# The h projections of a hybrid encoder layer as Strassen pairs, with raw gates and queries kept in DRAM

## The chip, the cores and the metric

The kernel runs on one core of a Trainium2 chip. The metric is the device time of one execution in microseconds. All arithmetic that decides the result is float32: every large matrix product is made of three float32r matmuls (high part times high part, high times low, low times high), so each operand is first split into a high part (a copy to float32r) and a low part (the original minus the high part).

## The reference, cut to what matters

One layer, sequence 1024, width 1024:

```python
h = rms_norm(x, g_pre)
proj = h @ w_in          # 7424 columns = 58 tiles of 128
(a_b, a_c, a_x, a_z, b_q, b_k, b_v, b_z, m_q, m_z, gate_logits) = split(proj)
ya = short_gated_conv(a_b, a_c, a_x, w_conv) * silu(a_z);          ua = ya @ w_up_a
yb = window_attention_with_sink(rope(q), rope(k), v) * silu(b_z);  ub = yb @ w_up_b
ym = memory_cross_attention(m_q, mk, mv) * silu(m_z);              um = ym @ w_up_m
merged = g0 * ua + g1 * ub + g2 * um       # g = sigmoid(gate_logits), 3 x 1024 channels
out = x + rms_norm(merged @ w_out, g_post)
```

Every product must keep float32 quality. The 58 tiles of `h @ w_in` are three quarters of the large matmuls; three up projections (24 tiles with half the depth) and the output projection (8 blocks) are most of the rest.

## The kernel before, in words

Everything is written out by hand: each engine has one in-order program, and semaphores tie them together. There is no planner and no due time; the place of an instruction in its engine's program is its priority.

Channels lie on partitions, positions along the free axis. `h_hi` and `h_lo` hold the normalized input for all of the kernel's first 920 us. A tile of 128 output channels is computed by `product` (L360 to L383): for both halves of the sequence and each of the eight chunks of the depth it issues three matmuls (L377, L378, L379), 48 in all, into `pm[:, p]`, one of two PSUM tiles. The weights of a tile arrive in `raw[:, p]` (512 KB), ScalarE makes the high part (`split_next`, L635 to L638) and GpSimd the low part (`low_part`, L336 to L341, the subtraction is L340), both a whole tile ahead of TensorE.

The stages come in this order: transposition of the normalized x under the first tile (`turn_x`, L398); K, V and four Q tiles, with rotation on VectorE (L944 to L947); 16 conv tiles (`conv_tiles`, `conv_z`, VectorE lines L961 to L978); eight rounds of `merge_a`, each a gate tile and an up tile with two groups of window attention among the matmuls (scores L458 and L459, `softmax_head` L1011, `softmax_tail` L1024 to L1027, transposition of the probabilities L466, `take_probs` L746 and L1034, values L480); z and memory queries; keys and values of the memory (L541, L555); eight rounds of `merge_b` with the cross-attention; the z and gate tiles of the third branch; and eight output blocks (`out_block`, L617 to L619). A gate tile is used at once: its sigmoid is taken from PSUM, and VectorE multiplies it with the up tile that follows. Queries, keys and values stay in SBUF. What VectorE and ScalarE take from PSUM they take a tile at a time (128 x 1024).

SyncE issues nearly all DMAs in order: weights, x, the swapped rows of one attention block at a time (`move_qk`), and the output. VectorE's program in `merge_a` and ScalarE's program in `merge_a` are one fixed sequence per round.

## Time and profile before

| | us |
|---|---|
| time, median of 3 runs (1020.91 to 1022.86) | 1021.28 |
| the profiled execution, its own time | 1020.34 |
| its span | 1018.3 |

| engine | busy, us | share of the span |
|---|---|---|
| TensorE matmul (PE) | 990.7 | 97% |
| weight load (PEld) | 824.7 | 81% |
| VectorE (DVE) | 474.3 | 47% |
| ScalarE (ACT) | 347.5 | 34% |
| GpSimd (POOL) | 167.6 | 16% |

The span is the time from the first to the last instruction of the profiled execution; the time of the execution is 2.0 us longer. Matmuls are pipelined, so the busy time of one overlaps the next: the distance between the starts of two of them, not the duration, is what one costs. An engine's busy time includes time in which an instruction has started and is held up.

### The profile page before, as it was taken

The numbers are of one execution on the slowest core, as the hardware profiler recorded it, in microseconds if no ns is written. First come the engines' busy times: TensorE is split into PE (matmuls) and PEld (weight loads), VectorE is DVE, ScalarE is ACT, GpSimd is POOL, SyncE is SP. The second block draws the span as 40 slices with busy tenths as digits, with TensorE's granted clock in tenths as the row PEclk, the third lists the DMA queues.
The fourth block names the chain that finished last, engine by engine and source line by source line (L and its number), as shares of the span: only waits on it lengthen the run. The fifth ranks groups of instructions, "written<-read, shape, count | busy, mean of one in ns | idle before, by whom it ended". The sixth has DMA issues, their size and how long they took to land.

```text
span 1018.3 us, 12976 instructions
## 1 busy us (share of the span) xinstructions
PE 990.7 (97%) x4672; PEld 824.7 (81%) x4672; DVE 474.3 (47%) x896; ACT 347.5 (34%) x567; POOL 167.6 (16%) x85
## 2 busy tenths in 40 slices
PE   4999999999999999999999999999999999999997
PEld 3788888888878888888888888888888888887885
DVE  5524322245477777774555544334435312127343
ACT  6321131211365555553320344434422211115121
POOL 1112122121111111111220011121122112210000
PEclk9999999999999999999999999999999999999999
DMA  6322111112111111111121410011111111160322
GB/s 224 107 51 53 62 41 62 41 41 70 32 50 50 50 49 49 49 39 62 41 84 62 135 62 31 31 51 38 44 42 45 49 31 62 31 257 0 124 82 83
DMA packets 21339, 65.41 MB, mean 64 GB/s; under 512 B 3232, under 2 KB 4384, under 8 KB 21056
## 3 DMA queue, kind: packets, MB, share of 16 engines
q1 hardware_dynamic: 20992, 64.39, 19.0%
q10 hardware_dynamic: 320, 0.66, 0.4%
q8 instruction: 18, 0.29, 0.1%
q14 instruction: 9, 0.07, 0.0%
HBM read 56.51 MB, written 4.19 MB: 60 GB/s over the span
## 4 chain that ended last, share of the span: by engine, by line
PE 84%; DVE 7%; ACT 4%; issue 3%; DMA 1%; DVEq 0%; SPq 0%; ACTq 0%
PE pm L377 22%; PE pm L379 22%; PE pm L378 22%; PE pm L617 3%; PE pm L619 3%; PE pm L618 3%; ACT area_a L738 2%; PE sa L466 2%; PE pv L589 1%; PE pm L541 1%; PE sa L573 1%; PE pv L480 1%; DVE area_a L1027 1%; DVE units_r L1034 1%; PE sa L458 1%
## 5 line engine op out<-in xcount | busy, mean ns | idle before, releaser
L377 PE MATMUL pm<-h_hi,units_r 128*128 128x512 f32 x928 | 364.0, 392 | 3.0 <-DVE h_lo L935 2.8
L379 PE MATMUL pm<-h_hi,units_r 128*128 128x512 f32 x928 | 361.7, 390 | 0.0
L378 PE MATMUL pm<-h_lo,units_r 128*128 128x512 f32 x928 | 361.7, 390 | 0.0
L340 POOL TENSOR_TENSOR units_r<-units,units_r 128x1024 fp32r<-128x1024 f32 x80 | 166.4, 2080 | 731.9 <-ACT units_r L638 731.9
L377 PEld LDWEIGHTS pm<-h_hi,units_r 128*128 128x128 f32 x928 | 174.5, 188 | 39.3 <-DVE h_lo L935 3.4
L379 PEld LDWEIGHTS pm<-h_hi,units_r 128*128 128x128 f32 x928 | 174.5, 188 | 36.5
L378 PEld LDWEIGHTS pm<-h_lo,units_r 128*128 128x128 f32 x928 | 174.6, 188 | 35.2
L638 ACT ACTIVATE units_r<-units 128x1024 fp32r<-128x1024 f32 x90 | 91.7, 1019 | 198.1 <-PE pm L379 172.2
L1179 DVE TENSOR_TENSOR area_a<-area_a,pm 128x1024 f32<-128x1024 f32 x15 | 18.3, 1221 | 139.5 <-PE pm L379 139.5
L377 PE MATMUL pm<-y_hi,units_r 128*128 128x512 f32 x192 | 76.9, 401 | 0.0
L379 PE MATMUL pm<-y_hi,units_r 128*128 128x512 f32 x192 | 75.0, 390 | 0.0
L378 PE MATMUL pm<-y_lo,units_r 128*128 128x512 f32 x192 | 74.8, 390 | 0.0
L617 PE MATMUL pm<-h_hi,units_r 128*128 128x512 f32 x128 | 50.0, 391 | 0.3 <-DVE h_lo L1226 0.2
L618 PE MATMUL pm<-h_hi,units_r 128*128 128x512 f32 x128 | 49.9, 389 | 0.0
L619 PE MATMUL pm<-h_lo,units_r 128*128 128x512 f32 x128 | 49.8, 389 | 0.0
L379 PEld LDWEIGHTS pm<-y_hi,units_r 128*128 128x128 f32 x192 | 36.0, 188 | 7.7
L1034 DVE TENSOR_TENSOR units_r<-sa,area_a_r 128x512 fp32r<-128x512 f32 x48 | 30.2, 684 | 24.9 <-ACT area_a_r L746 24.9
L378 PEld LDWEIGHTS pm<-y_lo,units_r 128*128 128x128 f32 x192 | 36.1, 188 | 6.7
L377 PEld LDWEIGHTS pm<-y_hi,units_r 128*128 128x128 f32 x192 | 36.1, 188 | 6.7
L746 ACT ACTIVATE area_a_r<-sa 128x512 fp32r<-128x512 f32 x48 | 25.2, 599 | 41.1 <-PE sa L466 41.1
L738 ACT ACTIVATE area_a<-area_a,st 128x384 f32<-128x384 f32 x64 | 38.4, 602 | 0.0
L837 ACT ACTIVATE area_a<-pm 128x1024 f32<-128x1024 f32 x8 | 8.2, 1027 | 74.5 <-PE pm L379 74.5
(154 smaller groups left out, 1037.9 us busy)
## 6 DMA issues: line engine op xcount, KB each, us to landing
units<-in_w SPq DMA_DIRECT2D x58, 512.0 KB, 3.3
units<-in_wup SPq DMA_DIRECT2D x24, 256.0 KB, 2.6
area_m<-in_x SPq DMA_DIRECT2D x8, 512.0 KB, 7.0
units<-in_wmem SPq DMA_DIRECT2D x8, 512.0 KB, 3.2
area_a<-in_wout SPq DMA_DIRECT2D x2, 2048.0 KB, 10.5
units<-in_x SPq DMA_DIRECT2D x8, 512.0 KB, 3.9
out<-area_a SPq DMA_DIRECT2D x7, 512.0 KB, 2.9
area_a_r<-area_m SPq DMA_DIRECT2D x16, 128.0 KB, 2.3
```

What stands on the lines that cost most here:

```text
L340: nc.gpsimd.tensor_tensor(w_lo[:, p, 0:width], raw[:, p, 0:width], w_hi[:, p, 0:width].bitcast(F32), ALU.subtract).then_inc(lo_made, 1)
L377: pe.matmul(pm[:, p, cols], hi, src_hi[:, k, cols], start=(k == 0), stop=False)
L378: pe.matmul(pm[:, p, cols], hi, src_lo[:, k, cols], start=False, stop=False)
L379: mm = pe.matmul(pm[:, p, cols], lo, src_hi[:, k, cols], start=False, stop=(k == chunks - 1))
L466: mm = pe.transpose(sa[:, bank, h * P:(h + 1) * P], probs[:, h, j * P:(j + 1) * P], ident[:, :])
L617: pe.matmul(dst, hi, wo_hi[:, n * HALF:(n + 1) * HALF], start=(k == 0), stop=False)
L618: pe.matmul(dst, lo, wo_hi[:, n * HALF:(n + 1) * HALF], start=False, stop=False)
L619: mm = pe.matmul(dst, hi, wo_lo[:, n * HALF:(n + 1) * HALF], start=False, stop=(k == KC - 1))
L638: nc.scalar.activation(w_hi[:, p, 0:width], raw[:, p, 0:width], ACT.Copy).then_inc(hi_made, 1)
L738: ins = nc.scalar.activation(probs[:, h, :], probs[:, h, :], ACT.Exp, bias=st[:, 3, h:h + 1], accum_out=st[:, 5, h:h + 1])
L746: nc.scalar.activation(probsT_hi[:, j, :], sa[:, bank, :], ACT.Copy).then_inc(pt_hi_made, 1)
L1034: nc.vector.tensor_tensor(probsT_lo[:, j, :], sa[:, bank, :], probsT_hi[:, j, :].bitcast(F32), ALU.subtract).then_inc(pt_lo_made, 1)
```

## The change

The projections of h are computed in pairs of tiles. A pair is a product of a 2x2 block matrix of weights (two tiles, each cut at half the depth: A11, A12 for the first, A21, A22 for the second) with a 2x2 block matrix of h (depth cut in two, sequence cut in two). Strassen's scheme in Winograd's form needs seven block products in place of eight. Each block product is 4 chunks times 3 matmuls of 128x512, so 12 matmuls. The 58 tiles make 29 pairs.

- h is kept as seven blocks `hc`, four of them sums (T1 to T4), each with high and low part; they are made once, after x is transposed. VectorE makes the sums, ScalarE the high parts, GpSimd and VectorE the low parts.
- Per pair, GpSimd makes four sums of weight blocks (S1, S3 in the place of A21, S2, S4), 128x512 each, and seven low parts; ScalarE seven high parts. The ring holds four operands, so operand n+4 may be made once product n is done.
- Seven PSUM results per pair, each a bank (128x512), are combined into four output blocks: ScalarE copies the first (`take_a`), VectorE adds the others with seven instructions that read PSUM.
- The order of work is new: K, Q and V pairs; z, gate and memory-query pairs for all branches, with the 16 groups of window attention one per pair in pairs 4 to 19; 16 memory steps; then the eight conv pairs, with the eight rounds of cross-attention one per pair; then all 24 up projections; then the output blocks, as before.
- Raw gates, raw z tiles and raw memory queries (pairs 3 to 20) are stored in DRAM and read back; rotated q and k, and the outputs of both attentions, too. SyncE issues all of it in order.

The products of a pair run in the order P1, P2, P6, P7, P4, P5, P3. TensorE puts the values of attention group gr - 1 (and of cross round i - 1) ahead of P2, the scores ahead of P6, and the transposition of the probabilities ahead of P3. ScalarE makes the high part of operand n + 4 after product n, and then runs `exps` after P6 and `take_probs` after P5. VectorE's program for one pair is, in order:

- after P1: `rotate` (pairs 2 and 3), `take_output(gr - 1)`, `conv_b`, `stage_mq(i)`;
- after P2: `take_c11`, `softmax_head(gr)` or `take_cross`, `cross_max(i)`;
- after P6: `add_p6`, then `rope_low`, `conv_y`, or in pair 20 `scale_mem`;
- after P7: `add_p7`, then `rotate`, `softmax_tail(gr)` or `cross_norm(i)`;
- after P4: `take_c21`, in pair 20 `split_mem`; after P5: `take_c22` and one more addition, `take_probs(gr)`; after P3: `take_c12`, then `conv_taps` in every second conv pair.

```diff
+HC = KC // 2
+H_OF = {"P1": B11, "P2": B21, "P3": B22, "P4": T4, "P5": T1, "P6": T2, "P7": T3}
+W_OF = {"P1": A11, "P2": A12, "P3": S4, "P4": A22, "P5": S1, "P6": S2, "P7": A21}
+def slot_order():
+    order = [(0, "P1"), (0, "P2"), (1, "P1"), (1, "P2")]
+    order += [(p, name) for p in range(2) for name in ("P6", "P7", "P4", "P5", "P3")]
+    for p in range(2, PAIRS):
+        if p == P_CONV:
+            order += [("m", i) for i in range(M_STEPS)]
+        order += [(p, name) for name in ("P1", "P2", "P6", "P7", "P4", "P5", "P3")]
...
@@ block.gpsimd
+            for n in range(8, NS):
+                p, name = ORDER[n]
+                low_part(n)
+                if name == "P3" and p < P_LAST:
+                    sums_first(p + 1)
+                elif name == "P1":
+                    sum_s2(p)
+                elif name == "P2":
+                    sum_s4(p)
...
@@ block.tensor
+            def product(n, moving_hi, moving_lo, bank, ready=None):
+                pe.wait_ge(hi_made, n + 1)
+                pe.wait_ge(lo_made, n + 1)
+                for k in range(HC):
+                    pe.matmul(bank, hi, moving_hi(k), start=(k == 0), stop=False)
+                    pe.matmul(bank, hi, moving_lo(k), start=False, stop=False)
+                    mm = pe.matmul(bank, lo, moving_hi(k), start=False, stop=(k == HC - 1))
...
@@ block.scalar
+            def high_part(n):
+                wait_operand(act, n)
+                at_least(act, slot_done, n - RING + 1)
+                nc.scalar.activation(ring[:, n % RING, 0, :], operand(n), ACT.Copy).then_inc(hi_made, 1)
...
@@ block.vector
+            def take_c21(p):
+                wait_slot(dve, p, "P4")
+                dve.wait_ge(c_made, p + 1)
+                nc.vector.tensor_tensor(raw_block(p, 1, 0), bank_of(p, "P4"), snaps[:, 2, :], ALU.add).then_inc(c21, 1)
...
@@ block.sync
+            for g in range(UPS):
+                if g >= 2:
+                    load_gate(g)
+                if g + 4 < UPS:
+                    sp.wait_ge(lo_made, NS + g + 1)
+                    sp.dma_start(spots[:, g % 4, :], wup[g + 4]).then_inc(spot_landed[g % 4], 16)
+                if g < 2:
+                    load_y(g + 2)
```

## Rows read from the trace of the kernel before

**Rows 1.** The page: span, busy time, and the chain by engine.

```profile
span 1018.3 us, 12976 instructions
PE 990.7 (97%) x4672; PEld 824.7 (81%) x4672; DVE 474.3 (47%) x896; ACT 347.5 (34%) x567; POOL 167.6 (16%) x85
...
PE 84%; DVE 7%; ACT 4%; issue 3%; DMA 1%; DVEq 0%; SPq 0%; ACTq 0%
```

**Rows 2.** Windows: stretch, its length, PE busy (count), clock, DMA share, GB/s.

```profile
26.50:72.10 45.60, 45.58 (x221) 1.00 0.26 80
...
480.00:560.00 80.00, 80.00 (x363) 1.00 0.20 66
640.00:700.00 60.00, 60.00 (x316) 1.00 0.12 39
```

**Rows 3.** Timeline of PE, 472 to 480 us: start, duration, line.

```profile
472.43 0.40 PE L377 MATMUL pm<-h_hi,units_r 128*128 128x512 f32 x1
...
479.92 0.39 PE L377 MATMUL pm<-h_hi,units_r 128*128 128x512 f32 x1
```

**Rows 4.** Windows of one attention round, all engines: PE PEld DVE ACT POOL.

```profile
304.00:329.51 25.51, 25.27 (x127) 20.94 (x126) 19.54 (x63) 14.70 (x31) 3.68 (x2) 1.00 0.19 50
```

**Rows 5.** Chain in order of time, near 60 us: start, length, what.

```profile
60.36 0.87 PE sa L431 x8
```

**Rows 6.** Groups by form: busy us, mean ns | idle before, releaser.

```profile
L340 POOL TENSOR_TENSOR units_r<-units,units_r 128x512 fp32r<-128x512 f32 x23 | 29.7, 1289 | 75.1 <-ACT units_r L638 75.1
...
L638 ACT ACTIVATE units_r<-units 128x512 fp32r<-128x512 f32 x8 | 5.0, 631 | 4.7 <-PE pm L379 4.7
...
L1034 DVE TENSOR_TENSOR units_r<-sa,area_a_r 128x512 fp32r<-128x512 f32 x48 | 30.2, 684 | 24.9 <-ACT area_a_r L746 24.9
L1027 DVE TENSOR_SCALAR area_a<-area_a,st 128x384 f32<-128x384 f32 x64 | 22.5, 416 | 0.6
```

**Rows 7.** Timeline of POOL and DVE near 204 us.

```profile
203.86 2.40 POOL L340 TENSOR_TENSOR units_r<-units,units_r 128x1024 fp32r<-128x1024 f32 x1 [6.22 <-ACT units_r L638]
...
202.83 1.23 DVE L961 TENSOR_TENSOR area_m<-pm,area_m 128x1024 f32<-128x1024 f32 x1 [13.77 <-PE pm L379]
204.18 2.63 DVE L963 TENSOR_SCALAR area_m<-area_m,wconv 128x1024 f32<-128x1024 f32 x1
```

**Rows 8.** Timeline of POOL and DVE near 795 us.

```profile
795.12 1.28 POOL L340 TENSOR_TENSOR units_r<-units,units_r 128x512 fp32r<-128x512 f32 x1 [8.41 <-ACT units_r L638]
...
784.69 3.10 DVE L1106 TENSOR_TENSOR area_a<-area_a 128x1024 f32<-128x1024 f32 x1
795.51 1.97 DVE L1106 TENSOR_TENSOR area_a<-area_a 128x1024 f32<-128x1024 f32 x1 [0.16 <-DVE area_a L1103]
```

**Rows 9.** Timeline, 8 to 12 us: two DVE instructions and one of POOL.

```profile
8.27 1.42 DVE L921 TENSOR_SCALAR area_m<-area_m,st 128x1024 f32<-128x1024 f32 x2
...
11.31 3.50 DVE L921 TENSOR_SCALAR area_m<-area_m,st 128x1024 f32<-128x1024 f32 x2
11.45 2.80 POOL L340 TENSOR_TENSOR units_r<-units,units_r 128x1024 fp32r<-128x1024 f32 x1 [11.00 <-ACT units_r L638]
```

**Rows 10.** Timeline of POOL and DVE near 317 us; ACT and DVE of one softmax.

```profile
316.05 2.39 POOL L340 TENSOR_TENSOR units_r<-units,units_r 128x1024 fp32r<-128x1024 f32 x1 [20.64 <-ACT units_r L638]
317.33 1.89 DVE L1034 TENSOR_TENSOR units_r<-sa,area_a_r 128x512 fp32r<-128x512 f32 x3 [1.63 <-ACT area_a_r L746]
...
322.09 0.60 ACT L738 ACTIVATE area_a<-area_a,st 128x384 f32<-128x384 f32 x1
324.61 0.58 ACT L752 COPY area_a<-pv 64x512 f32<-64x512 f32 x1
...
327.54 1.41 DVE L1027 TENSOR_SCALAR area_a<-area_a,st 128x384 f32<-128x384 f32 x4
```

**Rows 11.** DMA issues: size and median time from issue to landing.

```profile
units<-in_w SPq DMA_DIRECT2D x58, 512.0 KB, 3.3
units<-in_wup SPq DMA_DIRECT2D x24, 256.0 KB, 2.6
```

More of the change, by code:

```diff
@@ L18 @@
-from contextlib import ExitStack, contextmanager
+from contextlib import ExitStack
 import numpy as np
@@ L86, in link @@
     def link(self, ins):
[L88 removed]
+        self.count += 1
         ins.then_inc(self.sem, 1)
[L90 to L103 removed]
+        self.eng.wait_ge(self.sem, self.count)
@@ L436, in conv_tile, with turn_v @@
-            def conv_tile(j, q, first=0, last=None):
-                product(2 * j + (T_CONV + q) // 2, q % 2, KC, h_hi, h_lo, 4 * j + (T_CONV + q + 1), first, last)
-            with pe.Fori(0, AC - 1) as j:
-                for q in range(4):
-                    conv_tile(j, q)
-            def scores(i, g):
+            def turn_v(half):
+                pe.wait_ge((c11, c12)[half], 3)
+                if half == 0:
+                    pe.wait_ge(h_copied, 2 * KC)
+                for b in range(4):
+                    mm = pe.transpose(sa[:, half, b * P:(b + 1) * P], raw_block(2, 0, half)[:, b * P:(b + 1) * P],
+                                      ident[:, :])
+                mm.then_inc(v_turned, 1)
@@ L625, in _ @@
-            out_block(0, 1)
-            with pe.Fori(1, NB // 2 - 1) as i:
-                for p in range(2):
-                    out_block(i, p)
-            out_block(NB // 2 - 1, 0)
-            out_block(NB // 2 - 1, 1, last=True)
+                        hi, lo = mb[:, p, 0, k, :], mb[:, p, 1, k, :]
+                        wo = wo_of[half]
+                        pe.matmul(dst, hi, wo[:, k, 0, :], start=(k == 0), stop=False)
+                        pe.matmul(dst, lo, wo[:, k, 0, :], start=False, stop=False)
@@ L633, in _ @@
+                        mm = pe.matmul(dst, hi, wo[:, k, 1, :], start=False, stop=(k == KC - 1))
+                    if half == 0 and b == NB - 1:
+                        mm.then_inc(out_half_done, 1)
+                mm.then_inc(out_done, 1)
+            for b in range(NB):
+                out_block(b)
         @block.scalar
         def _(act):
-            def split_next(p, t_half, width=D):
-                act.wait_ge(raw_landed[p], 16 * t_half + 16)
-                nc.scalar.activation(w_hi[:, p, 0:width], raw[:, p, 0:width], ACT.Copy).then_inc(hi_made, 1)
@@ L888, in _ @@
-            with act.Fori(1, NB // 2 - 1) as i:
-                for p in range(2):
-                    out_block(i, p, True)
-            out_block(NB // 2 - 1, 0, False)
-            out_block(NB // 2 - 1, 1, False, last=True)
         @block.vector
@@ L1190, in merge_b, with cross_norm @@
                                         ALU.mult).then_inc(mnm_ready, 1)
-                if after is not None:
-                    stage_mq(after)
+            def cross_norm(i):
                 dve.wait_ge(mexped, i + 1)
```

2010 lines of the change are left out of this document (1192 added, 818 removed).

## The prediction

> **What bounds the kernel now.** I read the page first, then windows, then TensorE's own timeline, then what GpSimd and VectorE do to one another. The page gives TensorE 97% busy and 84% of the chain [rows 1]. Busy is no proof, since matmuls overlap, so the windows come next: whole stretches have PE busy for every microsecond of their length at the full clock [rows 2]. The timeline gives the price: from 472.43 to 479.92 there are 33 steps from start to start, 7.49 / 33 = 0.227 us for a 128x512 matmul, and no step longer than that [rows 3]. A tile of 48 costs 10.88. The kernel is TensorE's issue rate almost everywhere; the other engines have 50% and more to spare [rows 1]. A change that removes matmuls gains exactly what it removes, if all that now has to be ready for each product is ready.
>
> **What is removed.** 58 tiles x 48 = 2784 matmuls become 29 x 7 x 12 = 2436. 348 x 0.227 = **-79 us**. Up projections, output blocks, memory products, scores, transpositions and values keep their numbers. This is the full prize, 7.7%.
>
> **What is added, per pair.** TensorE: 84 x 0.227 = 19.0. GpSimd: seven low parts and four sums of 128x512, 11 x 1.29 [rows 6] = 14.1; in an old round of 25.5 us it had 3.7 [rows 4]. VectorE: seven additions from PSUM at 0.68 (row of L1034) [rows 6] = 4.8. ScalarE: seven copies at 0.63 [rows 6] and one from PSUM, 5.0. Sums of busy time all fit below 19. In an attention pair the group adds to TensorE what it did before: an old round is 72 h and up matmuls, 16.3 us, of 25.51 [rows 4], so 4.6 for a group with its waits, and the pair is 23.6. Throughput alone hides everything. What decides is latency in VectorE's fixed order, and there the trace has something that the old kernel could ignore.
>
> **The lock.** At 204.18 a 128x1024 tensor_scalar of VectorE on SBUF data takes 2.63 us; the GpSimd subtraction that started at 203.86 ends at 206.26, and only 0.55 is left after it [rows 7]. At 795.51 an SBUF-only tensor_tensor takes 1.97, where GpSimd's 128x512 instruction of 1.28 started just ahead of it; at 784.69, in the same step of a tile with a 128x1024 low part, it takes 3.10 [rows 8]. Operations that read PSUM go through untouched: L1034 at 317.33 needs 1.89 for three inside a GpSimd instruction [rows 10]. So a VectorE instruction that reads only SBUF waits for the whole GpSimd instruction. And it goes in turns: with nothing in the way two tensor_scalars take 1.42; at 11.31 two take 3.50, while GpSimd's 11.45 start takes 2.80 in place of 2.39, that is 0.41 to wait for the first of them, and then the second waits for all of GpSimd's [rows 9]. If GpSimd has a queue of work, each SBUF-only VectorE instruction costs its own time plus up to 1.29.
>
> The Trainium skill says the same (SBUF — State Buffer, "Who interferes with whom"): a VectorE instruction with two SBUF inputs, or in a two-port mode, and a GpSimd instruction that reads SBUF exclude each other for their full length. By that page the tiny 128x4 tensor_tensor at the head of `softmax_tail` is held too; the trace of before has none of them beside a GpSimd instruction. By the rule the stall below is 3.4 a pair, without it 1.9.
>
> **Attention pairs (16).** Time 0 is the end of P2. TensorE: scores to 1.4, with a wait for the first mask (VectorE has `take_c11`, 0.7, ahead of it) to 1.8; P6 to 4.5, P7 to 7.2, P4 to 10.0, P5 to 12.7, and then the transposition of the probabilities wants `p_ready`. ScalarE: after P6 a high part to 5.2, then the exponentials, 322.09 to about 324.6 in the old trace, 2.5 [rows 10], so exped at 7.8. VectorE: `add_p7` to 8.05, then `softmax_tail`. GpSimd in that stretch: low part of P3 5.3 to 6.6, S1 to 7.9, S3 to 9.25, and behind it without a gap the low part of P1, S2, the low part of P2, S4, the low part of P6: eight instructions in a row. The tail's four tensor_scalars, 1.41 together when free [rows 10], 0.35 each, now alternate with them: if the 128x4 operation is free, 9.25 + 4 x 0.35 + 3 x 1.29 = 14.5; if it is held too, one more turn, 16.1. TensorE stands from 12.7 to there: 1.9 or 3.4. Lower bound 0 (VectorE keeps the lock for all four), upper 4.8 (the reciprocal also takes a turn). I take 2.6, the middle of the two cases that the rows allow: 16 x 2.6 = **+42** (0 to 77). The mask wait is about the old round's bubbles and is not counted again. Behind the stalled transposition only P3 waits on TensorE; on VectorE `take_c21` and `take_c22` come late, but their banks are wanted three products on.
>
> **The opening, pairs 0 to 3.** Before, four tiles were done at 72.1: tile 2 ends at 60.36, then 0.87 and one tile [rows 5]. After, seven blocks of h must be made. GpSimd has ten low parts of them, nine operands and the sums of two pairs, in one order: P2 of pair 0 can start only after 4 block lows and 5.5 us of such work; P6 of pair 0 needs all of h, then VectorE's twelve SBUF additions of 0.7, then their high and low parts; from there each product needs two block lows and one low part of GpSimd, 3.9 us against 2.7. I get P6 of pair 0 at 49, P3 of pair 0 at 68, pair 1 at 85. That is 13 behind the old kernel where 5 ahead would be the full gain: 18. Pairs 1 to 3 then carry five rotations of three 1.2 us SBUF operations and one low part each, all under the lock, and each waits for four row DMAs that SyncE starts only when the tile is complete (an old load of 256 KB takes 2.6 [rows 11]): VectorE gets behind by a product or two and TensorE waits for banks, 5 to 8 more. From the bound where only the GpSimd rate counts to one where every rotation is a full turn late: 10 to 30; I take **+22**.
>
> **The memory steps.** `scale_mem` in pair 20 is five tiny operations and two tensor_scalars beside the same GpSimd queue, wanted 2.7 after P6: 7 late at worst. The 16 steps need a copy, a low part and a load each of about 1.4 in turn with TensorE. +6 (0 to 12).
>
> **The conv pairs (8).** `cross_norm` is four tensor_scalars in the same place: 1.7 late. In every second pair `conv_y` (two SBUF operations) is ahead of it: 4. `conv_taps` (four SBUF operations, 4.4 free, two or three turns held) stands ahead of `stage_mq`, and the next scores wait for that behind P2, 7.2 after P3: 2 late, three times. Together up to 27; if turns are lost only half the time, 13. **+20** (4 to 35).
>
> **The end.** Loads of z and attention output for the third y tile wait for `y_lo_made`, and the gate load stands behind them in SyncE's order. ScalarE takes that gate's sigmoid before the y tile's: up projection 4 starts about 5 late. One or two more after the last up. **+7** (2 to 14). The stores to DRAM lie beside other work: a pair moves 1 MB of weights and 1 MB of raw blocks in 19 us, about 110 GB/s; 80 GB/s took a share of 0.26 of the DMA engines [rows 2], so this would be some 0.36.
>
> **Sum.** 1018.3 - 79 + 42 + 22 + 6 + 20 + 7 = 1036.3 of span. The profiled execution's own time is 2.0 above its span and the median 0.9 above that: **1039**.
>
> **The rivals.** (a) The lock is taken once and kept: VectorE's queued instructions follow one another, so a tail waits once and ends at 10.7, before TensorE wants it. Then attention costs 0, conv 7, the opening 18, the memory steps 4 and the end 5: 1021 - 79 + 34 = 976. If a tail still loses one turn of 1.29 in half of the 27 places where one can, and attention's first mask 0.45 in 16, it is 976 + 17 + 7 = 1000. Between them, nearer the second, **993**. For it: the alternation rests on one place [rows 9]. Against it: there GpSimd plainly got in between. This one is faster; it decides at about 1.3 us of stall per attention pair, where the sum meets 1021. (b) Everything is hidden as the busy sums suggest and only the opening costs its lower bound: 1021 - 79 + 10 = **952**. For it: busy sums below 19 per pair. Against: the order. (c) More turns are lost than I count (reciprocal held, `take_c12` late, TensorE's clock falling in gaps: matmuls now never leave 1.00 in the windows [rows 2]): attention +77 and opening +30 in the sum above: 1039 + 35 + 8 = **1082**.
>
> **Chances.** Forecast 0.54 (1018 to 1076), (a) 0.28, (b) 0.05, (c) 0.13. Range: from 982 to 1080. The forecast's own range is 1018 to 1076. A measurement here can tell 0.2% from no change: 1019.2 to 1023.3 is same, 0.04, mostly from the bottom of the forecast. Faster 0.32, slower 0.64.
>
> **What would show it.** In the trace after: the transposition of the probabilities idle for 2 to 3 us each of 16 times, released by `softmax_tail`'s tensor_scalar; that instruction's mean well above 0.42, with GpSimd instructions between its four; pair 1 complete near 85 us, pair 4 near 135; gaps ahead of cross scores in every second conv pair; a gap of some 5 us at the fifth up. Wrong would be: tensor_scalars of the tail at 0.35 with GpSimd at work (then the lock is no matter), PE without gaps from 100 to 800 us, or gaps released by GpSimd itself, whose 14.1 a pair would then be longer than I read it.

## The result and the profile after

| | before | after |
|---|---|---|
| median of four runs, us | 1021.25 (1020.91 to 1022.86) | 1063.94 (1063.22 to 1065.82) |
| span of the profiled execution, us | 1018.3 | 1064.0 |
| ratio | | 1.0418, 95% interval 1.0400 to 1.0436 |

The kernel got 4.2% slower, by 42.7 us. The forecast was 1039 us, 1.7% slower, by 18: the direction and the range held, the size did not. Of the executions of all kernels in this document one, of the first run of section 7, was slow (1201 us at a granted clock of 0.745); it is in that run's median, and the ratios leave it out.

The page after, in the lines that answer to [rows 1], with the row of TensorE's granted clock in 40 slices of the span:

```profile
span 1064.0 us, 12467 instructions
...
PE 942.7 (89%) x4324; PEld 774.2 (73%) x4324; DVE 648.7 (61%) x1012; ACT 385.7 (36%) x736; POOL 542.0 (51%) x386
...
PEclk9778898999999999999999999999999798999999
...
PE 27%; DVE 10%; issue 4%; DMA 2%; ACT 2%; POOL 1%; SPq 0%; DVEq 0%; ACTq 0%
```

348 matmuls are gone, and TensorE is no longer busy all the time. The chain says less than it seems to: the profile follows it back only to 569 us, and its shares add up to 46% of the span, so TensorE's 27% is some 59% of what was followed, where before it had 84 of 99. No other engine is busy for more than 61%. So the question is who makes TensorE wait. The table of TensorE's waits from 28 us on (who waits, for whom: us in total, times, longest) answers it:

```profile
PE pm L675 <- POOL ring L589: 31.0, 8, 10.6
PE sa L740 <- DVE area L1369: 15.2, 16, 1.5
PE pm L907 <- DVE area L1591: 14.8, 2, 8.2
PE sa L818 <- DVE area L1421: 8.1, 8, 1.7
PE pm L675 <- DVE area L1240: 8.0, 2, 7.7
PE pm L907 <- POOL ring L589: 4.0, 3, 3.1
PE sa L810 <- DVE area_r L1407: 3.7, 3, 1.2
PE sa L732 <- DMA area_r<-kl_d: 3.7, 1, 3.7
PE pm L937 <- DVE hc L1580: 3.5, 1, 3.5
PE sa L784 <- DVE area_r L1398: 3.3, 1, 3.3
PE sa L732 <- DVE st L1354: 3.1, 15, 0.2
...
```

L675 is the first matmul of an h product, L907 of an up projection, L937 of an output block; L740 and L818 are the transpositions of the probabilities (attention, cross-attention), L732 and L810 the scores, L784 a memory step. Before, the same view from 28 us on has 4.8 us in all. Read by stage, TensorE waited 39 us and more for the h products of the opening, 18 in attention and 22 at the end.

The turns of the two engines are there as the forecast read them from [rows 7 to 9]. Timeline of VectorE and GpSimd at the tail of one softmax:

```profile
248.46 0.15 DVE L1366 TENSOR_TENSOR st<-st 128x4 f32<-128x4 f32 x1
248.65 0.18 DVE L1367 RECIPROCAL st<-st 128x4 f32<-128x4 f32 x1
248.86 5.25 DVE L1369 TENSOR_SCALAR area<-area,st 128x384 f32<-128x384 f32 x4
...
247.15 1.30 POOL L602 TENSOR_TENSOR spots<-spots 128x512 f32<-128x512 f32 x1
248.53 1.29 POOL L604 TENSOR_TENSOR spots<-spots 128x512 f32<-128x512 f32 x1
249.78 1.41 POOL L589 TENSOR_TENSOR ring<-spots,ring 128x512 fp32r<-128x512 f32 x1
251.15 1.40 POOL L610 TENSOR_TENSOR spots<-spots 128x512 f32<-128x512 f32 x1
252.51 1.39 POOL L589 TENSOR_TENSOR ring<-spots,ring 128x512 fp32r<-128x512 f32 x1
253.86 1.39 POOL L618 TENSOR_TENSOR spots<-spots 128x512 f32<-128x512 f32 x1
```

Four tensor_scalars that took 1.41 us [rows 10] take 5.25, one for each boundary between two of GpSimd's instructions. The groups by line (busy, mean ns); the first had a mean of 416 in [rows 6]:

```profile
L1369 DVE TENSOR_SCALAR area<-area,st 128x384 f32<-128x384 f32 x64 | 83.3, 1360 | 0.6
...
L1421 DVE TENSOR_SCALAR area<-area,st 128x256 f32<-128x256 f32 x32 | 36.9, 1213 | 0.3
```

In the opening and at the end the timeline (PE, then DVE, then POOL) shows longer gaps, and matmuls 0.43 us apart behind them instead of 0.23:

```profile
53.89 0.77 PE L675 MATMUL pm<-hc,ring 128*128 128x512 f32 x1 [10.62 <-POOL ring L589]
54.45 0.63 PE L676 MATMUL pm<-hc,ring 128*128 128x512 f32 x1
54.88 0.63 PE L677 MATMUL pm<-hc,ring 128*128 128x512 f32 x1
...
59.19 13.58 DVE L1302 TENSOR_TENSOR hc<-area,hc 128x512 fp32r<-128x512 f32 x8
115.31 1.23 DVE L1322 TENSOR_TENSOR area<-area 128x1024 f32<-128x1024 f32 x1 [8.05 <-DMA area<-area]
824.04 1.23 DVE L1567 TENSOR_TENSOR area<-area 128x1024 f32<-128x1024 f32 x1 [9.57 <-DMA area<-ob_d]
844.83 1.37 DVE L1569 TENSOR_TENSOR area<-area,snaps 128x1024 f32<-128x1024 f32 x1 [8.02 <-ACT snaps L1145]
...
97.27 1.26 POOL L602 TENSOR_TENSOR spots<-spots 128x512 f32<-128x512 f32 x1 [8.09 <-DMA spots<-in_w]
```

L1302 is a low part of a block of h, L1322 a rotation that waits for its swapped rows, L1567 and L1569 a y tile at the end, L602 the first weight sum of a pair. The gap of 10.62 is the one ahead of P6 of pair 0.

### The profile page after: what moved, and what is told of

It reads as the page before. It is cut to its first block and busy times, and to the rows that moved or that the text cites. A ratio compares the mean times of both kernels' runs of the same rounds, so it can differ in the third digit from the quotient of the medians.

```text
span 1064.0 us, 12467 instructions
## 1 busy us (share of the span) xinstructions
PE 942.7 (89%) x4324; PEld 774.2 (73%) x4324; DVE 648.7 (61%) x1012; ACT 385.7 (36%) x736; POOL 542.0 (51%) x386
## 5 line engine op out<-in xcount | busy, mean ns | idle before, releaser
L589 POOL TENSOR_TENSOR ring<-spots,ring 128x512 fp32r<-128x512 f32 x227 | 323.8, 1429 | 319.9 <-ACT ring L952 319.7
L675 PE MATMUL pm<-hc,ring 128*128 128x512 f32 x812 | 326.9, 403 | 40.2 <-POOL ring L589 31.0
L676 PE MATMUL pm<-hc,ring 128*128 128x512 f32 x812 | 321.3, 396 | 0.0
L677 PE MATMUL pm<-hc,ring 128*128 128x512 f32 x812 | 320.9, 395 | 0.0
L952 ACT ACTIVATE ring<-spots 128x512 fp32r<-128x512 f32 x227 | 141.9, 629 | 331.4 <-PE pm L677 299.6
L675 PEld LDWEIGHTS pm<-hc,ring 128*128 128x128 f32 x812 | 156.0, 192 | 75.9 <-issue 34.5
L677 PEld LDWEIGHTS pm<-hc,ring 128*128 128x128 f32 x812 | 155.4, 191 | 33.8
L676 PEld LDWEIGHTS pm<-hc,ring 128*128 128x128 f32 x812 | 156.0, 192 | 30.3
L907 PE MATMUL pm<-hc,ring 128*128 128x512 f32 x192 | 78.4, 409 | 18.8 <-DVE area L1591 14.8
L1369 DVE TENSOR_SCALAR area<-area,st 128x384 f32<-128x384 f32 x64 | 83.3, 1360 | 0.6
L908 PE MATMUL pm<-hc,ring 128*128 128x512 f32 x192 | 77.6, 404 | 0.0
L909 PE MATMUL pm<-hc,ring 128*128 128x512 f32 x192 | 77.3, 402 | 0.0
L907 PEld LDWEIGHTS pm<-hc,ring 128*128 128x128 f32 x192 | 37.8, 197 | 28.6 <-issue 20.8
L937 PE MATMUL pm<-hc 128*128 128x512 f32 x128 | 49.9, 390 | 3.5 <-DVE hc L1580 3.5
L938 PE MATMUL pm<-hc 128*128 128x512 f32 x128 | 49.8, 389 | 0.0
L939 PE MATMUL pm<-hc 128*128 128x512 f32 x128 | 49.8, 389 | 0.0
L602 POOL TENSOR_TENSOR spots<-spots 128x512 f32<-128x512 f32 x29 | 41.7, 1439 | 13.2 <-DMA spots<-in_w 13.0
L1136 ACT ACTIVATE area<-area 128x1024 f32<-128x1024 f32 x24 | 25.4, 1057 | 62.8 <-DMA area<-raw_d 62.8
L1240 DVE TENSOR_TENSOR area<-pm,snaps 128x512 f32<-128x512 f32 x29 | 20.0, 690 | 42.4 <-PE pm L677 35.7
L1251 DVE TENSOR_TENSOR snaps<-pm,snaps 128x512 f32<-128x512 f32 x29 | 20.0, 689 | 40.8 <-PE pm L677 40.6
L1245 DVE TENSOR_TENSOR snaps<-pm,snaps 128x512 f32<-128x512 f32 x29 | 20.0, 691 | 39.6 <-PE pm L677 39.1
```

The lines of the kernel that those rows point to most:

```text
L589: nc.gpsimd.tensor_tensor(ring[:, n % RING, 1, :], operand(n), ring[:, n % RING, 0, :].bitcast(F32), ALU.subtract).then_inc(lo_made, 1)
L675: pe.matmul(bank, hi, moving_hi(k), start=(k == 0), stop=False)
L676: pe.matmul(bank, hi, moving_lo(k), start=False, stop=False)
L677: mm = pe.matmul(bank, lo, moving_hi(k), start=False, stop=(k == HC - 1))
L907: pe.matmul(dst, hi, y[:, at, 0, cols], start=(begin and c == chunks[0]), stop=False)
L908: pe.matmul(dst, hi, y[:, at, 1, cols], start=False, stop=False)
```

## The experiments

Every one starts from the changed kernel. A ratio is to the kernel before on the same chip, where the changed kernel stands at 1.0418; the times of single events are those of the profiled execution. TensorE's first scores start at 164.09 us in the changed kernel and its up projections, from the last values of the cross-attention (806.64) to the end of the last (966.55), take 159.9 us, where 24 x 24 matmuls at 0.227 are 130.8. Both vary where the edit doesn't touch them: in the eight profiled executions that have the changed kernel's opening as it is, the first scores start between 160.7 and 164.1, and in seven that have its end as it is, the up projections take 159.7 to 164.0. Differences inside of these spreads are read as none.

### 1. The divisions by the softmax sum on ScalarE

```diff
@@ softmax_tail, VectorE
-    for h in range(GROUP):
-        ins = nc.vector.tensor_scalar(probs[:, h, :], probs[:, h, :], st[:, 6, h:h + 1], None, ALU.mult)
@@ ScalarE, after P7
+    for h in range(GROUP):
+        ins = nc.scalar.activation(probs[:, h, :], probs[:, h, :], ACT.Identity, scale=st[:, 6, h:h + 1])
```

> The four tensor_scalars that divide the probabilities by their sums move from VectorE to ScalarE (activations with a scale), where nothing takes turns with GpSimd's weight sums. Theory (turns with the weight sums): in the changed kernel those four take 5.25 us from the first to the last where VectorE's own pace was 416 ns each, and TensorE stands 0.92 us at the transposition and 0.2 us at the scores in each of 16 attention pairs; with them gone the pairs lose that, so about -19 us, period 24.81 -> about 23.6 us, and GpSimd's low sums beside them fall from about 1.40 to 1.29 us. Rival (the stall is the order or the latency of the chain, not the turns): the activation takes its own time behind the exponentials and the high sums, so the stall stays or grows, 0 to +10 us.

Measured: 1048.49 us, ratio 1.0263 (1.0226 to 1.0300); span 1044.3, so 19.7 less. The transposition waits for nothing any more, while each operation takes 606 ns on ScalarE against 1360 in turns (groups by line):

```profile
L1045 ACT ACTIVATE area<-area,st 128x384 f32<-128x384 f32 x64 | 34.2, 606 | 0.3
L741 PE MATMUL sa<-ident,area 128*128 128x128 f32 x192 | 23.6, 272 | 0.0
```

The turns held TensorE in the attention pairs. They cost 15.2 us of waits, 15.5 in the median times and 19.7 in the spans of the two profiled executions, so 15 to 20 us. The 0.2 us at the scores (3.1 in all) stayed.

### 2. GpSimd's weight sums 4 columns wide

```diff
-    nc.gpsimd.tensor_tensor(spots[:, S1, :], spots[:, A21, :], spots[:, A22, :], ALU.add)
+    n = HALF if p == 0 else 4
+    nc.gpsimd.tensor_tensor(spots[:, S1, 0:n], spots[:, A21, 0:n], spots[:, A22, 0:n], ALU.add)
```

and the same for S3, S2 and S4.

> GpSimd's four weight sums of a pair cover 4 columns in place of 512 for pairs 1 to 28 (the products of those pairs are not the reference's; all else runs as before). Theory (what is slow in the changed kernel is VectorE taking turns with GpSimd, whose work the sums have grown from 2 to 3 operations of 1.3 us a product's worth): the 16 attention pairs lose their 0.92 and 0.2 us stalls (-18), the conv pairs part of 15.6 us (-8 to -12), the opening and the end little (0 to -6): -26 to -36 us. Rival (the turns are with the low parts of the weights, which stay, and the sums only stand beside them): 0 to -8 us, the 0.92 us stalls stay.

Measured: 1042.05 us, ratio 1.0197 (1.0163 to 1.0230); span 24.1 less, where 26 to 36 were expected. With seven low parts and no sums in a pair, the tail's mean fell to half and TensorE's wait for it from 15.2 to 0.5; the first scores start at 161.7, and the up projections did not get shorter:

```profile
L1369 DVE TENSOR_SCALAR area<-area,st 128x384 f32<-128x384 f32 x64 | 40.1, 687 | 0.6
```

So the sums make the attention stall, the low parts alone don't. Of the 24 us, 15 are that wait and 6 the same wait in the conv pairs (8.1 to 1.7); in the opening and at the end no cost of the sums shows.

### 3. The conv pairs

```diff
@@ cross_norm: as in experiment 1, on ScalarE
@@ VectorE, after P1
     if 1 <= i:
         stage_mq(i)
+    if 1 <= i < NB - 1 and i % 2 == 1:
+        conv_taps(p - 1)
@@ VectorE, after P3
-    if 0 <= i < NB - 2 and i % 2 == 0:
-        conv_taps(p)
```

> In the eight conv pairs the four tensor_scalars that divide the cross attention's probabilities (2.7 us for two in turns with GpSimd, 349 ns each before) move to ScalarE, and the raw query's staging goes ahead of the convolution's taps on VectorE. Theory (turns at the division, staging behind the taps): the 1.24 us gaps ahead of the scores and the 0.65 to 1.24 us gaps ahead of the transposition go, 15.6 us of loss falls to 3 to 6: -9 to -13 us. Rival (VectorE's sum of work in turns fills those pairs, so a gap moves to another wait): -3 to +3 us.

Measured: 1054.43 us, ratio 1.0326 (1.0309 to 1.0344), span 11.4 less; the time fell by 9.5, as the theory had it. Between 614 and 800 us TensorE waited 10.0 us in the changed kernel; here it is this (waits):

```profile
PE pv L831 <- issue: 0.8, 1, 0.8
PE sa L819 <- ACT area L1065: 0.3, 1, 0.3
```

### 4. TensorE's clock kept up

```diff
+BUSY_OPEN = {(0, "P2"): 28, (0, "P6"): 44, (0, "P5"): 30, (2, "P1"): 24, (3, "P1"): 20}
+BUSY_UP = {2: 34, 4: 26, 11: 0}
+    def keep_busy(count, bank, idx):
+        for _ in range(count):
+            pe.matmul(bank, hc[:, idx, 0, 0, 0:P], hc[:, idx, 0, 0, :], start=True, stop=True)
```

> TensorE is given matmuls without use (28, 44, 30, 24, 20 of them, 128x512) in five of the opening's gaps and two (34 and 26) in the up projections' gaps, before the matmul that waits; nothing else changes and their results are not read. Theory (part of the loss is TensorE at the lower of its clock levels after each gap: about 62 us of its work run at the lower level, 31 us of which would not be spent at the full one): the granted clock stays near 1 behind those gaps, matmuls 0.217 instead of 0.43 us apart, and the kernel gets up to 31 us shorter, half of that if VectorE or GpSimd end the next wait anyway: -10 to -31 us. Rival (VectorE and GpSimd bound those stretches, the slow matmuls were hidden behind them): the gaps grow by what the clock gives back, -3 to +3 us.

Measured: 1064.96 us, ratio 1.0414 (1.0393 to 1.0435): nothing. The clock did stay up in most of the gaps (page), and behind such a gap the matmuls are 0.23 apart (timeline); the first scores at 161.0 are within the spread:

```profile
PEclk9999998999999999999999999999999899998999
...
101.14 0.47 PE L677 MATMUL pm<-hc,ring 128*128 128x512 f32 x1 [0.79 <-POOL ring L591]
101.45 0.40 PE L678 MATMUL pm<-hc,ring 128*128 128x512 f32 x1
101.68 0.40 PE L679 MATMUL pm<-hc,ring 128*128 128x512 f32 x1
```

In the changed kernel TensorE is busy for some 47 us at the lower of its two levels (the expectation had 62), here for some 30, and the time did not follow. The waits come back at the next operand: P7 of pair 0 waits 2.23 us for GpSimd at 59.30, where it waited 0.58. The theory, 10 to 31 us, falls; a gain of a few us, hidden in the runs' spread, is not ruled out.

### 5. The opening: three orders and one size

Loads and rotations in another order:

```diff
@@ VectorE, pairs 2 and 3: rotate(j) of side 1 moves from P1 to P2, behind take_c11
@@ SyncE: load_spot(A22, 2) and load_spot(A22, 3) go ahead of swap_rows
```

> In the opening, VectorE rotates the second halves' queries after the results of the odd block product are taken instead of ahead of them (there it stood 8.05 and 7.99 us for the DMAs that swap the rows), and the loads of pair 2's and pair 3's last weight blocks are issued ahead of SyncE's row swaps (GpSimd waited 8.09 us for the first of them). Theory (a transfer issued late, behind a wait on its queue, makes half of the opening's gaps): the gaps of 6.04 and 5.04 us ahead of pairs 2 and 3 fall away, and with them the half-speed stretches behind them (about 3.4 us of work each), so -12 to -20 us. Rival (in the opening only the turns of VectorE and GpSimd count; both engines have more work than TensorE there): the gaps come back later, -3 to +3 us.

Measured: 1067.42 us, ratio 1.0445 (1.0417 to 1.0472). A gap of 6.10 us is back at 105.99, the others became 1.82 and 2.20. The first scores at 161.2 are within the spread, so nothing was won. The rival was right.

All low parts of the combinations on VectorE:

```diff
@@ GpSimd: low_of_combination(T2, T3, T4, T1, B22; j = 0, 2) removed
@@ VectorE
-    for j in (1, 3):
+    for j in range(HC):
         low_of_combination(nth + 1, idx, place, j)
```

> In the opening VectorE forms all low parts of the five combinations of h (20 in place of 10), GpSimd none. With the two engines taking turns a pair of such operations takes 1.71 us (1.29 of them GpSimd's), while VectorE alone starts one every 0.60 us. Theory (between 51 and 73 us the turns set the pace): VectorE's stretch of 21.7 us (14 operations, each with one of GpSimd's) becomes 24 x 0.60 plus turns with four low parts of weights, about 17 us, so the 7.73 us gap ahead of the second pair shrinks by 4 to 5 us; -4 us for the kernel, -8 with what follows at the higher clock level. Rival (the products of pair 0 wait for each combination's low part on one engine longer): 0 to +5 us.

Measured: 1067.34 us, ratio 1.0456 (1.0437 to 1.0474). The gap grew from 7.73 to 13.17; it stands ahead of P5 of pair 0, which waits for VectorE's addition of pair 1's first result (L1240). GpSimd, free of its low parts, went on to the next pair's sums (L602 to L618), and VectorE took turns with those: 1.21 us a piece in place of the 0.60 that I had reckoned with (timeline):

```profile
56.51 19.41 DVE L1302 TENSOR_TENSOR hc<-area,hc 128x512 fp32r<-128x512 f32 x16
...
64.72 1.70 POOL L602 TENSOR_TENSOR spots<-spots 128x512 f32<-128x512 f32 x1
66.51 1.59 POOL L604 TENSOR_TENSOR spots<-spots 128x512 f32<-128x512 f32 x1
```

ScalarE's rounding of the rotated tiles later, on top of the first of these orders:

```diff
@@ ScalarE: rope_high of side 1 from P2 to P6, of side 0 from P7 to P4; rope_high(0) from P6 to P7
@@ VectorE: rope_low and the second rotate, SyncE: store_rope, one or two products later too
```

> In the opening, on top of the rotations and loads in the other order (that run gained 2.9 us at the first scores), ScalarE rounds the rotated tiles one or two products later, VectorE and SyncE follow. There ScalarE stood 8.15, 6.35, 9.53 and 8.62 us at a rotated tile, with the rounding of the next weights queued behind it, and GpSimd 6.67, 6.64 and 2.77 us for those. Theory (the coupling of the queues): the gaps of 6.15, 1.83, 2.61 and 1.14 us ahead of pairs 2 to 4 shrink to 0 to 2 in all, the first scores start at 152 to 156 us in place of 164, -8 to -12 us for the kernel. Rival (VectorE and GpSimd in turns, or the landing of the swapped rows, bound it): the gaps come back at another product, the first scores start at 160 or later, -4 to 0 us.

Measured: 1067.35 us, ratio 1.0456 (1.0438 to 1.0475), first scores at 162.29. The gap of 6.1 fell to 4.06, and a new one of 3.02 came from VectorE. The rival again: the gaps came back elsewhere, though the kernel got 3 us slower where it had 0 to 4 less.

The rotations 4 columns wide:

```diff
-    link(nc.vector.tensor_tensor(raw, raw, cosb, ALU.mult))
+    link(nc.vector.tensor_tensor(raw[:, 0:4], raw[:, 0:4], cosb[:, 0:4], ALU.mult))
```

and so the two others and the four transfers of swapped rows.

> In the changed kernel the five rotations of the key's and queries' tiles, and the transfers that swap their rows, cover 4 columns in place of 1024 (keys and queries are not the reference's); all waits and their order stay, and so do the two roundings and the stores. Theory (VectorE's 15 operations of 1.2 to 2.3 us, of which each also holds GpSimd's for a turn, set the pace of pairs 1 to 3): the gaps of 6.04 and 5.05 us shrink below 2 in all and their half-speed stretches go, first scores at 148 to 154 us in place of 164, -10 to -16 us. Rival (the fixed latency of the transfers and the queues' order, which 4 columns do not change): first scores at 160 or later, 0 to -4 us.

Measured: 1053.62 us, ratio 1.0324 (1.0308 to 1.0339), first scores at 150.80. The gaps of 6.04 and 5.05 are now 1.25 and 2.11, and TensorE's waits for GpSimd up to the first scores are these, against 31.0:

```profile
PE pm L675 <- POOL ring L589: 23.3, 7, 10.6
```

So the size of the rotations, on VectorE in turns and in the transfers, is worth 10 to 13 us of the opening (10.3 in the median times, 13.3 at the first scores, 9.9 against the earliest of the untouched openings), and the two orders tried are worth nothing. Whether VectorE's operations or the transfers make it, the run doesn't tell. The gaps of 10.6 and 7.7 us at 54 and 75 us were taken away by no run (those with the busy TensorE only filled them, and the low parts on VectorE turned 10.6 and 7.7 into 9.3 and 13.2). They stand where the seven blocks of h are made, ahead of P6 and of P5 of pair 0; what would shorten them stays open.

### 6. The end

The product with the gate ahead of the y tiles:

```diff
@@ VectorE: gate_up(g) ahead of y_tile and wo_low; ScalarE: y_tile a step later
@@ SyncE: load_gate(2), load_gate(3) ahead of load_y(2), load_y(3)
```

> At the end VectorE forms the gate times up tiles ahead of the output's y tiles rather than behind them, ScalarE's part of y comes a step later, and the loads of the third and fourth raw gates are issued ahead of the loads of y. Theory (the gaps of 8.21, 6.57 and 3.14 us in the up projections and the 14.5 us between them and 130.6 + 1 us are order: gate_up stands behind a y tile that waits for its own transfers): gaps and the half-speed work behind them go, -12 to -25 us. Rival (the transfers of raw gates and weights are short of DMA time there, whatever the order): -3 to +3 us.

Measured: 1083.16 us, ratio 1.0605 (1.0579 to 1.0631), 19 worse, outside of both. The first gaps got shorter (2.15, 3.15), but there are now six waits in the first branch, 17.9 us in all in place of two of 14.8, and three in the second, 15.1 in all, with 8.08 and 6.73 at 911 and 925. I read it so, and no run shows it: each load of y waits in SyncE's queue for a place that is now free a step later, and the next raw gate's load stands behind it.

The y tiles spread over the steps, and loads issued as early as their places allow:

```diff
 def y_step(g):
-    if g < AC:
-        return g
-    return g - 5 if KC < g <= KC + AC else None
+    return {1: 0, 2: 1, 4: 2, 6: 3, 9: 4, 10: 5, 12: 6, 14: 7}.get(g)
@@ SyncE: load_gate(0), load_gate(1), load_y(0), load_y(1) ahead of store_cross(NB - 1)
```

> At the end SyncE issues the raw gates' and y tiles' loads before it waits for the last cross output (they stood behind a wait that ended at 814.5 us, while their places were free at 808.4), and the eight y tiles are formed at up steps 1, 2, 4, 6, 9, 10, 12, 14 in place of 0 to 3 and 9 to 12, so that the first product with a gate no longer stands behind a y tile. Theory (order and latency of the raw tiles' way back: 27.5 us are lost in the up projections): the 8.21 us gap falls to 0 to 2, the 6.57 us gap goes, the 3.1 us gaps of steps 10 and 11 shrink; -14 to -22 us. Rival (the sum of transfers from 815 to 870 us is what takes the time, DMA share 0.6 to 0.9): the gaps come later, 0 to -5 us.

Measured: 1062.52 us, ratio 1.0392 (1.0369 to 1.0416). The 8.21 us gap is 0.69, and 3.15, 4.77, 2.81 us come later: up projections still 158, and 1.4 us less for the kernel where the theory had 14 to 22. That looked like the transfers.

28 loads narrow, those of the raw gates and of the raw factors of y; only the gates' are shown:

```diff
-    sp.dma_start(gate[:, g % 2, :], raw_d[GATE[g // KC] + g % KC - T_GA])
+    w = 2 * HALF if g < 2 else 64
+    sp.dma_start(gate[:, g % 2, 0:w], raw_d[GATE[g // KC] + g % KC - T_GA][:, 0:w])
```

> At the end the raw gates from the third on and the raw factors of y from the third on come back 64 columns wide in place of 1024 (28 loads of 512 KB less; what the up projections are multiplied with is not the reference's). All waits and their order stay. Theory (the time of the transfers that the change adds: seven spread-out y tiles gained nothing, so it isn't the y tiles' place): the up projections take 135 to 142 us in place of 158, -14 to -22 us for the kernel. Rival (order: a raw gate's load is issued only when a y tile's low part is made, and small transfers don't change that; or VectorE's and GpSimd's own work in turns): -2 to -6 us.

Measured: 1062.52 us, ratio 1.0394 (1.0368 to 1.0421), up projections 156.5. The up projections are some 3 us below the spread where 135 to 142 were expected, so the size of these transfers is not what holds them; the attention outputs' loads kept their size. What is left is order, or the engines' work in turns. SyncE's own waits in the run with the spread tiles say where (waits from 804 to 910 us):

```profile
SPq L529 <- POOL hc L654: 43.2, 6, 12.1
SPq L516 <- DVE area L1588: 16.6, 5, 7.3
```

L529 is `load_y`, waiting for a place of y; L516, `load_gate`, comes behind it in the queue, and waits for VectorE itself too.

Loads of y a step later still (steps 1, 2, 5, 6, 9, 10, 13, 14, loads two steps after a tile; the cut is against the spread tiles above):

```diff
-    if g and y_step(g - 1) is not None and y_step(g - 1) + 2 < 2 * AC:
-        load_y(y_step(g - 1) + 2)
+    if g >= 2 and y_step(g - 2) is not None and y_step(g - 2) + 2 < 2 * AC:
+        load_y(y_step(g - 2) + 2)
```

> As the run with the y tiles spread over the up steps, and on SyncE a y tile's load is issued a step later still (steps 3, 4, 7, 8, 11, 12), so that the wait for a place of y no longer stands ahead of the next raw gate's load: there SyncE stood from 816.9 to 826.4 us with gate 3 behind it, which landed at 835 and let VectorE wait 7.6 us. Theory (head of line on SyncE): the gaps of 3.15, 4.77, 2.81 us and those of 3.4 and 1.8 us at steps 9 and 10 shrink to half, up projections 145 to 150 us in place of 158: -8 to -13 us against the changed kernel. Rival (two places for raw gates, whose load starts only when VectorE has taken the gate two steps before, are too few beside 4.4 us a transfer, whatever the queue's order): -2 to +2 us.

Measured: 1060.23 us, ratio 1.0376 (1.0350 to 1.0402), up projections 152.7: 7 us less where 8 to 13 were expected, and half of that reached the kernel's time.

The three queues untied:

```diff
@@ VectorE
     if y_step(g) is not None:
         y_tile(y_step(g))
-    if wo_step(g) is not None:
-        wo_low(wo_step(g))
     gate_up(g)
+    if wo_step(g) is not None:
+        wo_low(wo_step(g))
@@ ScalarE: y's sigmoid, then wo_high, then y's rounding (was: sigmoid, rounding, wo_high)
@@ SyncE: wup[4], wup[5] ahead of load_y(0); the first y tiles at steps 2 and 3
```

> At the end, on top of the y tiles spread over the up steps and their loads a step later: VectorE forms the gate times up before the output weights' low part, ScalarE rounds the output weights before y, the weights of up steps 4 and 5 are loaded ahead of the y tiles (ScalarE waited 8.33 us for them with a y tile's sigmoid queued behind), and no y tile stands ahead of step 2. Theory (three in-order queues wait for each other in each step: y's sigmoid, y, its rounding, the output weights' rounding and low part, then the product with the gate): the gaps of 2 to 4.2 us fall to 0 to 1.5, the up projections take 136 to 145 us in place of 158, so -13 to -20 us. Rival (transfers of a raw gate with two places only): 150 us or more, -3 to -8.

Measured: 1049.96 us, ratio 1.0274 (1.0242 to 1.0307), up projections 142.3. TensorE's waits from 806 us on fell from 23.1 to 10.1:

```profile
PE pm L933 <- DVE hc L1581: 3.5, 1, 3.5
PE pm L903 <- DVE area L1594: 2.4, 1, 2.4
PE pm L903 <- DVE area L1592: 2.3, 3, 1.7
PE pm L903 <- POOL hc L657: 1.1, 2, 0.7
```

Here the theory holds, and its number too. The run holds the moved loads of the one before; against that run, 1060.23, it gained 10.3. It changes four things at once, and which of them counts no run tells.

### 7. Together

Experiments 1 and 3, the first of the opening and the fourth of the end:

> Together: the probabilities' division on ScalarE in the attention and conv pairs, the query's staging ahead of the taps, the opening's rotations and loads in the other order, and the end's order of the run beside it. If the parts add (-15.4, -9.5, -3 at the scores' start, and the end's): 1026 to 1034 us, so still no faster than the kernel before (1021); if the end's order takes 10 us too and the early gains are not eaten by it: 1022 to 1027. Rival (what is won early is lost at a later bound, as with the warm TensorE): 1040 or more.

Measured: 1025.03 us, ratio 1.0039 (1.0022 to 1.0055), in the range expected for an end worth 10 us, though the end gave some 7. By stage the parts add: from the first scores to the last values of the cross-attention the changed kernel takes 642.6 us, the run of experiment 1 17.6 less, that of experiment 3 13.2 less, this one 31.8 less, and the up projections take 152.1. In the median times the whole is more than the sum: 15.5, 9.5 and 3.7 make 28.7, and together it is 38.9. Where the other 10 come from is open.

The same with the fifth of the end in place of the fourth, and the later rounding in the opening:

> Everything together: the two divisions on ScalarE, the query staged ahead of the taps, and the two new orders of the opening and the end. The run before of this kind took 1025 us. Theory (the queues' coupling holds what was left): 7 to 10 us less at the first scores and 7 to 14 less in the up projections, so 1002 to 1012 us, faster than the kernel before (1021). Rival (VectorE's and GpSimd's sum of work in turns is the bound in the opening and at the end): 1018 to 1026 us.

Measured: 1019.55 us, ratio 0.9979 (0.9968 to 0.9989). The end gave its 10 us (142.4 for the up projections), as the theory had it; the opening gave nothing (first scores at 163.2), and the time lies in the rival's range.

And TensorE kept busy in four gaps of the opening:

> The run with everything together (1019.6 us), and TensorE kept busy with matmuls without use in four gaps of the opening (28, 44, 30 and 14). Theory (the level of TensorE's clock behind a gap counts where TensorE sets the pace; in the changed kernel it did so only in part of the opening, and the first scores came 3.1 us earlier): 1015 to 1018 us. Rival (VectorE's queue ends those stretches whatever TensorE's clock is): 1019 to 1021 us.

Measured: 1015.68 us (1013.69 to 1018.01), ratio 0.9943 (0.9928 to 0.9958), the fastest of all and 0.6% below the kernel before. The number is the theory's, and the two intervals do not meet. That the busy TensorE made the 3.9 us is not shown: the profiled executions, of which this one was the slowest of its six, have spans of 1016.2 and 1016.5, and their first scores stand at 162.3 and 163.2. In both these wait for the transfer of the keys, 6.2 and 5.6 us, and an earlier TensorE gains nothing at that point.

## Why the prediction was right and wrong

| term | forecast | in the trace |
|---|---|---|
| matmuls removed | -79 | -79; 0.23 apart where nothing stops them |
| opening | +22 | +50 to the end of P2 of pair 4, +54 with the wait for the keys |
| attention | +42 | +19 |
| memory steps | +6 | +6 |
| conv pairs | +20 | +15 |
| up projections | +7 (with the output) | +27 |
| output | | +3 |

The right column adds up, stage by stage, what the steps between the starts of two matmuls take above their usual length (0.227 us for 512 columns, 0.177 for 384, 0.120 for 256, 0.109 for 128), less the same sum in the trace of before: 158.3 us against 33.5. With the -79 it gives 45 to 46; the span grew by 45.7.

**Right.** The turns, their form and their places: the transposition stalls 16 times, the tail's tensor_scalars alternate with four of GpSimd's instructions, their mean is 1360 ns, and taking them off VectorE or taking the sums away ends the stall (experiments 1, 2). Conv pairs were sized within 5 us and have the two causes named, `cross_norm` and `stage_mq` behind the taps (experiment 3, which moved both at once). The memory steps are 6 as forecast; no run took them apart.

**Attention, too large by 23.** The term was mis-sized: a stall of 2.6 was the middle between 1.9 and 3.4. The 128x4 addition took 0.15 and cost no turn, so the case of 1.9 was the one; and in it the first tensor_scalar started 8.5 us after P2, one GpSimd instruction earlier than I had it (9.25), so the probabilities were ready at 13.8 and not at 14.5, with TensorE there at 12.9. That is 0.92, and the 0.2 for the mask. Why the addition cost nothing is a matter of where it fell: in 15 of the 16 tails it started within 0.02 us of the end of one GpSimd instruction and some 0.07 ahead of the next, as at 248.46 in the timeline above (L602 had ended, L604 started at 248.53). So the rule of the Trainium skill (SBUF — State Buffer, "Who interferes with whom"), by which a running GpSimd instruction would have held it, was not put to the test by these tails, and they do not speak against it.

**The opening, too small by 32.** The forecast had P6 of pair 0 at 49, P3 of pair 0 at 68, pair 1 done at 85 and pair 4 near 135. The trace has 53.9, 83.4, 97.1 and, for the end of P2 of pair 4, 160.4. The step that failed is "from there each product needs two block lows and one low part of GpSimd, 3.9 us": in the trace GpSimd takes 5.1 for the three, since each is in turns with VectorE (1.7 us in place of 1.3):

```profile
58.68 3.43 POOL L594 TENSOR_TENSOR hc<-area,hc 128x512 fp32r<-128x512 f32 x2
62.07 1.74 POOL L589 TENSOR_TENSOR ring<-spots,ring 128x512 fp32r<-128x512 f32 x1
63.76 3.45 POOL L594 TENSOR_TENSOR hc<-area,hc 128x512 fp32r<-128x512 f32 x2
```

And it left out that VectorE has 14 operations in that stretch (21.7 us from 51 to 73) with the drains of the PSUM banks queued behind them, so P5 of pair 0 lost 7.7. Up to the end of pair 1 the loss is 31 where 18 was forecast. From there to P2 of pair 4 it is 19; I had allowed 5 to 8 us for the rotations and then taken 22 for the whole, which leaves 4. Their size alone is worth 10 to 13 (experiment 5). The wait for the keys, 4 us, was not in the forecast. The prediction's own sign of being wrong, gaps released by GpSimd itself, is there: 31.0 us in eight waits, all in the opening. Not all of the cause is shown: no run took the gaps of 10.6 and 7.7 away.

**The end, too small by 23.** I had one gap of 5 us at the fifth up projection, from a gate load behind the loads of y. There are two, of 8.2 at the third and 6.6 at the fifth, and three behind them. The step that failed is that I followed SyncE's queue only, for one step. ScalarE's and VectorE's queues are tied as well, with the output weights' rounding and low part between a y tile and the product with the gate, in every step with a y tile: untying them together with SyncE's loads is worth 14 us, 10 of them beyond what the loads' order gave alone (experiment 6). The width of 28 of the loads isn't it.

**The clock.** The third rival named it. It fell at every gap of 5 us and more and at some of 3 to 4, and in the changed kernel it cost nothing that a run could show (experiment 4).

The errors had both signs: 28 too much for attention and conv pairs, 55 too little for the opening, the end and the output. That the measured time is within the range owes something to that luck: 28 us of span are left, where the opening and the end alone would have given 55.

## What to carry to other kernels

When a change loads a second engine beside VectorE, add up not its busy time but the boundaries between its instructions at which a VectorE operation on SBUF data can get in, and move short VectorE operations on the critical chain to ScalarE; two such moves, one of them with a reordering, gave back 25 us here. A stall found by following one in-order queue was a lower bound here, 7 us where 30 were lost: follow each of the queues that wait for each other around one full step before pricing it. And before blaming a low clock or a wide transfer for lost time, ask what TensorE would have waited for next: here neither gave back more than a few us. And a difference between two profiled executions counts only if it is larger than that stage's spread over the runs that leave it alone.

## What the runs showed of the hardware

- VectorE and GpSimd alternate one instruction at a time as long as both have work: from 59.19 on eight of VectorE's low parts took 13.58 us, 1.70 each, where such operations start 0.60 apart alone (43.28 and 43.88 in the same trace). GpSimd's instructions took some 1.7 us each there; over the whole kernel it pays less, 1429 ns in the mean for a low part against 1289.
- Small operations are held or not by what they read and where they fall. The 128x4 tensor_tensor of the 16 tails took 153 ns in the mean, but 15 of them started between two GpSimd instructions. The 128x4 reciprocal behind it, with one input in SBUF, started some 0.12 us into a GpSimd instruction in 15 tails and took 0.18 all the same. In the run with narrow rotations the one tensor_tensor of three that started while GpSimd was at work (from 87.19, for 1.30) was held to its end (timeline of VectorE and GpSimd):

```profile
87.02 0.16 DVE L1322 TENSOR_TENSOR area<-area 128x4 f32<-128x4 f32 x1
87.19 1.30 POOL L589 TENSOR_TENSOR ring<-spots,ring 128x512 fp32r<-128x512 f32 x1 [1.42 <-ACT ring L952]
87.22 1.28 DVE L1323 TENSOR_TENSOR area<-area 128x4 f32<-128x4 f32 x1
88.53 0.16 DVE L1324 TENSOR_TENSOR area<-area 128x4 f32<-128x4 f32 x1
```

- Behind gaps of 5 to 10 us TensorE runs at the lower of its two levels, 1.2 GHz, with matmuls 0.43 apart in place of 0.23 (behind the gap at 103.09 the granted clock was 0.62 in the mean from 104.5 to 109.5 us and 1.00 from 111 to 113). With matmuls without use in that gap it was 1.00 from 101.5 to 106.5, the level of 2.4 GHz.
